# One block for the first norm and the layer-0 input projection, one block for forgetting attention, in a hybrid decoder step

## The reference, cut to what matters

```python
def rmsnorm(x, g):
    y = xf * lax.rsqrt(jnp.mean(xf * xf, axis=-1, keepdims=True) + EPS) * g

mq, mk, mv, mo, mi, mf, fq, fk, fv, ff = _split(xn @ w_in, EVEN_COLS)   # 1024 -> 28 tiles of 128 and 16 gate columns

def fox_attend(q, Fq, tq, k, v, Fk, tk):
    s = einsum(q, k) * (F_DH ** -0.5) + Fq[..., :, None] - Fk[..., None, :]
    s = where(tk <= tq, s, -inf)
    return einsum(softmax(s), v)
```

## Time and profile before

| | |
|---|---|
| median of 3 runs | 1648.03 us (1643.51 to 1653.4) |
| the profiled execution | 1647.61 us |
| its span in the trace | 1645.8 us |
| mean granted TensorE clock over the span | 0.961 |
| TensorE busy | 1555.1 us, 94% |
| input block, to the first instruction of the norm | 0 to 19.6 us |
| norm and projection (28 tiles) | 19.6 to about 219 us |
| forgetting attention, three blocks | about 350 to 472 us |

### The profile page before, as it was taken

One profiled execution on the slowest core, in us unless ns is written; L12 is line 12 of the kernel. 1 busy time (PEld: TensorE's weight loads), 2 busy tenths in 40 slices (PEclk: granted clock), 3 DMA queues, 4 the chain that ended last, 5 costly groups with the idle time before them and its releaser, 6 DMA issues. The chain is left out here.

```text
span 1645.8 us, 31029 instructions
## 1 busy us (share of the span) xinstructions
PE 1555.1 (94%) x11869; PEld 1449.7 (88%) x11869; DVE 1002.6 (61%) x1667; ACT 627.1 (38%) x1106; POOL 289.6 (18%) x313
## 2 busy tenths in 40 slices
PE   7999989988889999999999899999898999999997
PEld 5999976666659899999999899987598999999996
DVE  5332364643645989888532677635659988886325
ACT  4111231434524445555421332236334355555211
POOL 1421000400000035444000000012200254441000
PEclk8999999879999999999999999999699999999999
DMA  5223133677452023333433222230430323325221
GB/s 146 81 79 90 51 97 92 214 224 240 133 175 76 26 78 103 102 91 89 114 85 89 84 74 78 91 103 3 121 91 12 92 78 103 102 76 141 73 68 55
DMA packets 225796, 161.14 MB, mean 98 GB/s; under 512 B 17885, under 2 KB 206025, under 8 KB 225696
## 3 DMA queue, kind: packets, MB, share of 16 engines
q1 hardware_dynamic: 222416, 157.94, 33.1%
q0 software_dynamic: 3280, 1.85, 0.5%
HBM read 150.13 MB, written 9.89 MB: 97 GB/s over the span
## 5 line engine op out<-in xcount | busy, mean ns | idle before, releaser
L2327 ACT CAST w_high<-ring 128x1024 fp32r<-128x1024 f32 (+1 forms) x68 | 81.5, 1199 | 315.0 <-PE psum L2045 306.8
L2638 DVE TENSOR_TENSOR w_low<-ring,w_high 128x1024 fp32r<-128x1024 f32 (+1 forms) x68 | 97.3, 1430 | 92.4 <-ACT w_high L2327 92.4
L2161 PE MATMUL psum<-t_high,piece_high 128*128 128x280 f32 (+1 forms) x512 | 149.0, 291 | 4.1 <-ACT first_product L2463 2.5
L2162 PE MATMUL psum<-t_low,piece_high 128*128 128x280 f32 (+1 forms) x512 | 148.5, 290 | 0.0
L2163 PE MATMUL psum<-t_high,piece_low 128*128 128x280 f32 (+1 forms) x512 | 148.1, 289 | 0.0
L2428 ACT CAST piece_high<-ring 128x512 fp32r<-128x512 f32 x160 | 98.7, 622 | 75.7 <-PE psum L2163 48.4
L2161 PE MATMUL psum<-b_high,piece_high 128*128 128x280 f32 (+1 forms) x384 | 111.8, 291 | 2.1 <-DVE hidden_b L2820 2.1
L2162 PE MATMUL psum<-b_low,piece_high 128*128 128x280 f32 (+1 forms) x384 | 111.6, 291 | 0.0
L2163 PE MATMUL psum<-b_high,piece_low 128*128 128x280 f32 (+1 forms) x384 | 111.3, 290 | 0.0
L2161 PEld LDWEIGHTS psum<-t_high,piece_high 128*128 128x128 f32 x512 | 96.4, 188 | 5.0 <-ACT first_product L2463 2.9
L2163 PEld LDWEIGHTS psum<-t_high,piece_low 128*128 128x128 f32 x512 | 96.5, 188 | 0.0
(11 more groups left out here) (562 smaller groups left out, 4576.8 us busy)
## 6 DMA issues: line engine op xcount, KB each, us to landing
ring<-in_ffn_wd SPq DMA_DIRECT2D x16, 1408.0 KB, 7.1
ring<-in_ffn_wg SPq DMA_DIRECT2D x40, 512.0 KB, 4.0
ring<-in_ffn_wu SPq DMA_DIRECT2D x40, 512.0 KB, 5.2
ring<-in_w_in_even SPq DMA_DIRECT2D x14, 1024.0 KB, 5.3
ring<-in_w_in_odd SPq DMA_DIRECT2D x12, 1024.0 KB, 5.2
ring<-in_cache_fox_k SPq DMA_DIRECT2D x44, 256.0 KB, 4.3
projected<-in_cache_fox_v SPq DMA_DIRECT2D x28, 256.0 KB, 3.1
projected<-in_cache_fox_k SPq DMA_DIRECT2D x20, 256.0 KB, 3.8
```

The source lines that it names most:

```text
L2161: mm(bank, wh[:, k], xh[:, k, :], start=(j in (0, 1, 3) and k == 0), stop=False, skip_group_check=True)
L2162: mm(bank, wh[:, k], xl[:, k, :], start=False, stop=False, skip_group_check=True)
L2327: nc.scalar.copy(dst, src).then_inc(w_hi[p], 1)
L2638: v.tensor_tensor(dst, src, high_.bitcast(F32), ALU.subtract).then_inc(w_lo[p], 1)
```

## The change

**First stage.** The norm and the two projections become one block. `norm` goes away, and `project` returns one program for each engine, which the block calls one after the other. ScalarE makes the eight high parts and two weight pieces, then all eight squares. VectorE makes the eight low parts and the two weight pieces, then adds the eight squares up into one chunk (seven additions). TensorE begins its first tile chunk by chunk as the parts come, does the second, then two matmuls with ones for the sums, then the third and the fourth. The first turn is written out, the loop begins with the second. GpSimd makes no squares. The eight constants are loaded at the head of this block instead of the input block. The waits for constants and gate weights, which stood at the end of SP's program in the norm block, now stand with GpSimd's gather and with ScalarE's and VectorE's use of the gate weights. The gate products go to banks 4 and 5, behind the last use of the third tile's banks; the third tile of `even_b` waits until they are read.

**Second stage.** The three blocks of forgetting attention become one. New semaphores take the place of the block ends: TensorE's first `scores` waits for the maxima in `rows_h`, the first product with values for the copied scores of the past and for the ones beside the values; `past_maximum` and SP's loads over the keys' place wait for the copied scores (`s_S`). The probabilities of the first group are turned before the values, those of the second between the fourth and the fifth page of the first group. VectorE copies the first group's probabilities ahead of its last reciprocal. `close_fox_sems` moves behind the whole.

The diff, cut to its core:

```diff
+            def tile(i, tl, as_normed=False):
+                slot, p = tl // 2, tl % 2
+                pe.wait_ge(low_done[p], i * 2 + (s0 + slot + 1))
+                pe.wait_ge(tile_free[tl], i + free0[tl])
+                if normed and tl == 3:
+                    pe.wait_ge(n_root2, 2)
+                if pe_first is not None and tl == 2:
+                    pe.wait_ge(s_gv, 1)
...
+                    if as_normed:
+                        pe.wait_ge(n_high, k + 1)
+                    for w, m, end in ((w_high, x_high, 0), (w_high, x_low, 0), (w_low, x_high, 1)):
+                        if as_normed and m is x_low:
+                            pe.wait_ge(n_low, k + 1)
...
+            if pe_first is not None:
+                pe.wait_ge(tile_free[2], free0[2])
+                pe_first(pe)
+            if normed:
+                tile(0, 0, True)
+                tile(0, 1)
+                pe.wait_ge(n_acc, KC - 1)
+                for half in range(2):
+                    nc.tensor.matmul(banks[6 + half][:, 0:HALF], ones[:, :], normed[:, 0, half * HALF:(half + 1) * HALF],
+                                     start=True, stop=True).then_inc(n_sum, 1)
+                tile(0, 2)
+                tile(0, 3)
+            with pe.Fori(start, iters) as i:
+                for tl in range(4):
+                    tile(i, tl)
...
+            if normed:
+                for k in range(KC):
+                    nc.scalar.mul(x(k)[0], h[:, k, :], gain(0, 0, k)).then_inc(n_high, 1)
+                    if k in (0, 3):
+                        split_high(act, 0, 0, k // 3)
+                for k in range(KC):
+                    nc.scalar.activation(normed[:, k, :], h[:, k, :], ACT.Square).then_inc(n_sqa, 1)
+                split_high(act, 0, 1, 0)
+                nc.scalar.activation(eps[:, 1:2], eps[:, 0:1], ACT.Sqrt)
+                split_high(act, 0, 1, 1)
+                for half in range(2):
+                    act.wait_ge(n_sum, half + 1)
+                    nc.scalar.activation(rstd[:, half * HALF:(half + 1) * HALF], banks[6 + half][:, 0:HALF],
+                                         ACT.Sqrt, bias=eps[:, 0:1], scale=1.0 / D).then_inc(n_root2, 1)
...
+            if normed:
+                for k in range(KC):
+                    dve.wait_ge(n_high, k + 1)
+                    x_high, x_low = x(k)
+                    v.scalar_tensor_tensor(out=x_low, in0=h[:, k, :], scalar=gain(0, 0, k), in1=x_high.bitcast(F32),
+                                           op0=ALU.mult, op1=ALU.subtract).then_inc(n_low, 1)
+                    if k in (0, 3):
+                        split_low(dve, 0, 0, k // 3)
+                for k in range(1, KC):
+                    dve.wait_ge(n_sqa, k + 1)
+                    if k > 1:
+                        dve.wait_ge(n_acc, k - 1)
+                    v.tensor_tensor(normed[:, 0, :], normed[:, 0, :], normed[:, k, :], ALU.add).then_inc(n_acc, 1)
+                split_low(dve, 0, 1, 0)
+                split_low(dve, 0, 1, 1)
+                for half in range(2):
+                    dve.wait_ge(n_root2, half + 1)
+                    v.reciprocal(rstd[:, half * HALF:(half + 1) * HALF], rstd[:, half * HALF:(half + 1) * HALF])
+                v.drain()
...
+
+    def load_constants(sp):
         for dst, name in ((tri_ts, "tri_ts"), (tri_st, "tri_st"), (small, "small"), (smask, "smask")):
...
     def gather_lf(pool):
+        pool.wait_ge(s_const, 16 * 8)
...
     def gate_weights_high(act):
+        act.wait_ge(s_gw, 16 * 7)
...
     def gate_weights_low(dve):
+        dve.wait_ge(s_gw, 16 * 7)
...
     def gate_products(pe):
+        pe.wait_ge(s_gl0, 1)
...
-                    last = nc.tensor.matmul(banks[6 + half][0:96, 0:HALF], w[:, k, :],
+                    last = nc.tensor.matmul(banks[4 + half][0:96, 0:HALF], w[:, k, :],
...
-    norm(None, None, (0, 0), proj[:, 0:KC * T].rearrange("p (k t) -> p k t", k=KC), xn, splitters(1, KC, pieces),
-         load_gate_weights, zero_gate_weights)
...
-    project(even_a, 1, 4, KC, chunk(xn), Pt, 0, pieces, then=even_b, beside=gather_lf, normed=True,
-            following=(1, KC, False), act_first=gate_weights_high, dve_first=gate_weights_low)
-    project(even_b, 1, 3, KC, chunk(xn), Pt, 16, pieces, beside=reorder_lf, scaled=True, split=True,
-            pe_first=gate_products, dve_first=gate_logits, act_last=(log_sigmoid_by_scalar, gates_by_scalar),
-            dve_last=(log_sigmoid_by_vector, gates_by_vector), dve_after=keep_cumulated, bank_free=(s_gv, 1))
+    sync_a, tensor_a, scalar_a, vector_a = project(
+        even_a, 4, KC, chunk(xn), Pt, 0, pieces, then=even_b, following=True, normed=Pt,
+        act_first=gate_weights_high, dve_first=gate_weights_low)
+    sync_b, tensor_b, scalar_b, vector_b = project(
+        even_b, 3, KC, chunk(xn), Pt, 16, pieces, pe_first=gate_products, dve_first=gate_logits,
+        act_last=(log_sigmoid_by_scalar, gates_by_scalar), dve_last=(log_sigmoid_by_vector, gates_by_vector),
+        dve_after=keep_cumulated)
+    with nc.Block() as block:
...
+        def _(sp):
+            load_constants(sp)
+            load_gate_weights(sp)
+            sync_a(sp)
+            sync_b(sp)
...
+        def _(pe):
+            tensor_a(pe)
...
+        def _(pool):
+            zero_gate_weights(pool)
+            gather_lf(pool)
+            reorder_lf(pool)
...
+            sp.wait_ge(s_S, 2)
+            load_v(sp, 25, 20)
...
+            sp.wait_ge(s_fp, 2 * 4 * per_pair)
+            load_v(sp, 55, 2)
+            sp.wait_ge(v_used, 3)
+            load_v(sp, AFTER_USE, 2 * 32 - AFTER_USE)
+            sp.wait_ge(v_used, PAGES)
+            prefetch(sp, out_even)
...
+            pe.wait_ge(s_less_max, 2)
+            scores(0)
...
+                if p == 0:
+                    pe.wait_ge(s_S, 2)
+                    pe.wait_ge(s_one, 1)
...
+            def probs_turned(g):
+                b0 = 4 * g
+                pe.wait_ge(s_x2, g + 1)
+                if g:
+                    pe.wait_ge(s_fo, 16)
+                    pe.wait_ge(s_fd, 16)
...
+            probs_turned(0)
+            for g in range(2):
+                for e in range(2):
+                    pe.wait_ge(s_t2c[e], g + 1)
+                for pg in range(PAGES + 1):
+                    values(g, pg)
+                    if g == 0 and pg == 3:
+                        probs_turned(1)
+                    if g and pg == 3:
+                        out_turned(0)
+            out_turned(1)
...
+                    if c == 3 and r == 1:
+                        probs_copied(0)
...
-    close_fox_sems()
-
```

More of the change, by code:

```diff
@@ new lines, in project @@
+    def project(unit, iters, kc, x, dst, first, pieces, then=None, following=None, normed=None, pe_first=None, act_first=None,
+                dve_first=None, act_last=None, dve_last=None, dve_after=None):
+        full0, free0 = list(full_n), list(free_n)
+        s0 = split_n[0]
+        split_high, split_low, part = splitters(1, kc, pieces)
+        high, low = pieces
+        sent[0] += 16 * iters
+        split_n[0] += 2 * iters
+        for tl in range(4):
+            full_n[tl] += iters
+            free_n[tl] += iters
+        next_high, next_low, _ = splitters(1, kc, pieces) if following else (None,) * 3
+        start = 1 if normed else 0
@@ new lines, in by_tensor @@
+        def by_tensor(pe):
+            def tile(i, tl, as_normed=False):
[6 more added lines that the diff above has]
+                    pe.wait_ge(s_gv, 1)
+                w_high, w_low = part(high, p), part(low, p)
+                for k in range(kc):
+                    x_high, x_low = x(k)
[5 more added lines that the diff above has]
+                        for half in range(2):
+                            last = nc.tensor.matmul(banks[2 * tl + half][:, 0:HALF], w[:, k, :],
+                                                    m[:, half * HALF:(half + 1) * HALF],
+                                                    start=(k == 0 and w is w_high and m is x_high),
+                                                    stop=(k == kc - 1 and end == 1))
+                last.then_inc(tile_full[tl], 1)
+            if pe_first is not None:
[11 more added lines that the diff above has]
+            with pe.Fori(start, iters) as i:
+                for tl in range(4):
+                    tile(i, tl)
@@ L502, in transposes @@
         tr_n[1] += len(jobs) // 2
-    (n_sqa, n_sqp, n_pair, n_sum, n_root, n_y, n_h, n_high, n_sq) = (sem(x) for x in (
-        "squares_by_scalar", "squares_by_gpsimd", "square_pairs", "sum_done", "root_done", "post_normed", "residual",
-        "x_high", "h_squares"))
-    n_root2 = sem("h_root_done")
-    roots = [0]
-    posts, pres = [0], [0]
-    def sums_of_squares(pe, sq, chunks, ready, base, first_bank, done=None):
-        for j in range(chunks):
-            pe.wait_ge(ready, base + j + 1)
-            for half in range(2):
```

(17 more changed lines are left out.)

716 lines of the change are left out of this document (249 added, 467 removed).

## The result

The changed kernel takes 1630.1 us in the median of eight runs (1628.5 to 1635.2), the kernel before 1651.3 in the median of all 76 runs on record (1643.0 to 1657.6). In the first comparison the ratio was 0.989, with a 95% interval of 0.9864 to 0.9917; in the second, with more runs of before, 0.9882 (0.9852 to 0.9913). So the change makes the kernel 1.1 to 1.2% faster. The forecast was 1622, the range 1615 to 1630: the direction was right, the time is 8.3 us over the forecast and 0.1 us outside the range, and the gain is 21.2 us where 26.2 were forecast.

The account below looks back on a forecast made before the run. TensorE, busy 94% of the span, sets the pace, so time is won where it idles or runs at its lower clock. Gains 10.5 + 5.9 + 5.4 + 4.4 = 26.2 from 1647.6 give 1621.4, called 1622 against the median; range 1615 to 1630.

Parts of the forecast that it names:

- Step 1: Norm and projection: first tile starts chunk by chunk, sums follow the second; fourth tile ends at 48.4, gain 10.5 us.
- the first tile did not crawl: Rival at the projection's start: waits in each chunk keep TensorE at 1.2 GHz into the second tile; 1627 us, chance 0.12.
- Step 2: Gate products between `even_a` and `even_b`: they follow the last tile without gap at full clock, gain 5.9 us.
- Step 3: Forgetting attention, entry into the softmax part: TensorE waits only for the maxima, no block end; gain 5.4 us.
- Step 4: Forgetting attention, samples' values: transposes follow the last product directly, so values begin earlier; gain 4.4 us.
- the rival taken from the Trainium skill: Forgetting attention: transposes let the clock fall, first group's values partly at half rate, 2 us lost; 1624 us, chance 0.08.
- a grant under 1.00 in the steady part: Rival over the whole span: longer unbroken work makes the chip grant less clock, say 1660 us; chance 0.02.
- the low ends: The four steps' smallest gains, 6.8 + 5.6 + 4.2 + 2 = 18.6 us, or 1629 us.

Follow-up runs that it names:

- start_warm7: The kernel before with only the first-stage change, and seven instead of four products of constants ahead of the mLSTM heads: 1634.6 us, ratio 0.9903 to before.
- `warm` runs: The changed kernel with five, six or seven instead of four products of constants ahead of the mLSTM heads: 1626.7, 1630.2 and 1626.0 us.
- held kernels: Both kernels with the mLSTM heads' tiles reordered and the row of four-column products split in two: changed kernel 1626.9 us, kernel before 1645.8 us.

## Why the prediction was right in its parts and wrong in its sum

**Step 1, the start: right.** 10.5 us were said, 58.92 - 47.43 = 11.5 came in the profiled pair, 1 us of it because the input block ended earlier in this execution (15.35 against 16.35). Over all profiles with the old start (five) and the new one (nine), the fourth tile is drained 57.3 - 47.2 = 10.1 us earlier. TensorE stood at the first product 1.6 us earlier than said, at 1.2 GHz as said (0.66 in the microsecond from 24, then 1.00). VectorE's additions ended at 30.7, ahead of the 33 said; the first tile did not crawl.

**Step 2, the gate products: right.** 5.9 said; the first drain of `even_b` is 17.45 us earlier, 6.0 more than the fourth tile. Over the same five and nine profiles, the gates come 199.7 - 184.1 = 15.6 us earlier, against 16.4 said for both steps.

**Step 3, the entry: right.** 5.4 said, 13.48 - 8.84 = 4.6 in the means of six and eight profiles. The step had ScalarE load its table right behind its copy; it loads it only when the first scores are there (386.27, 0.39 us idle), and TensorE waits 1.45 us for the exponential.

**Step 4, the samples' values: right.** 4.4 said; 82.85 - 78.13 = 4.7 in the means. The first values stand 2.0 us behind the start of the transposes, and no fall of the clock follows the transposes in that stretch, so the rival taken from the Trainium skill ("TensorE: Matmul & The Clock Gate", Part 4: PE-mode transpose) did not come; each group's transposes last only 1.2 us, so this tests that rule little. The prediction's own ground for counting transposes was misread: from the start of the input block TensorE multiplies constants, and it transposes only from 10.77 to 16.31. The granted clock stayed at 1.00 through those 5.5 us and fell at 18.82 (0.91 in the microsecond from 18), so the conclusion stands for them.

**The sum: wrong.** "10.5 + 5.9 + 5.4 + 4.4 = 26.2 from the profiled 1647.6" assumed that what the change doesn't touch takes as long as in that one execution. This term was put at nothing without a reason, and it is the step that failed. In the profiled pair the steps came to 17.5 + 4.8 + 3.3 = 25.6 us, and the rest took 8.4 more: 10.2 in the mLSTM heads and the block behind them, less what other stretches gave. No rival priced this: those on the clock asked about the first tile, the transposes and a grant under 1.00 in the steady part, and none of these came. The profiled execution of before was 3.7 us under the median of all runs, and its heads held a clock that the other five profiles without an edit there lost.

Against the medians, the 8.3 us between 1621.8 and 1630.1 have three parts. The base was 3.3 too low: three runs gave 1648.0, all 76 give 1651.3. The steps gave 15.6 + 4.6 + 4.7 = 24.9 in the means, 1.3 less than 26.2. And the medians lie only 21.2 apart, so 3.7 were lost in stretches that the change doesn't touch. Two of these are longer in the profiles of the changed parts. With unaltered heads, the heads and the block behind take 60.1, 55.8 and 60.1 with the new start, 49.9, 55.8 and 55.8 with the old one, and `start_warm7` and the `warm` runs show that what runs ahead of them changes this. From the out-projection to the end, the eight profiles with merged forgetting attention take 1159.1 to 1166.4, 1163.4 in the mean, the six without 1158.7 to 1162.3, 1161.0 in the mean; there the clock is at 1.2 GHz for 52.5 us in the shortest and 66.7 us in the longest. But these are few executions, and which pattern a run without a profile fell on isn't known, so how the 3.7 us divide stays open.

The range was also narrower above than its own working: the low ends gave 1629, and the 2 or 3 us that a median may be off, which were taken off below (1618 to 1615), would have made the upper end 1631 to 1632.

## What to carry to other kernels

A gain of known steps is to be subtracted from a median of many runs, not from one execution. A stage that the change doesn't touch can still move, if TensorE's clock there hangs on what ran before it: compare two executions of the same kernel before a difference in such a stage is laid to a change. Where a row of products with few columns stands in a full stretch, it is worth trying to split it and move the parts between large ones: here that gave 3 us in the changed kernel, while one large product set into the row gave nothing that can be told. A block's end that an engine off the path reaches last is worth about the wait in the timeline: here 4.6 us where TensorE had stood still for 5.0 (392.04 to 397.05), and 4.7 where it had stood for 4.34, there with a new order of the work beside it.

## What the runs showed of the hardware that was not expected

The granted clock fell with TensorE busy 12.10 of 12.10 us; each fall in the heads came within a row of products of four columns each or at most 0.9 us behind it. I had read the clock as a matter of stops. That the few columns are the cause is argued from this and from the held kernels, not shown by itself: seven constant products ahead of the heads held the clock in heads 1 and 2 with the rows as they were. The Trainium skill ("TensorE: Matmul & The Clock Gate", Part 1: The HAM clock gate, What's actually happening) says that what watches the engine runs on by itself and does not begin anew with a kernel, so that the point of change varies. The traces agree: the same 67 products a head took 10.1 to 13.1 us, and where unaltered heads began equally long (to 0.06 us) after the clock's last return, each head's time was the same to 0.06 us. And adding work ahead of a stage (seven constant products for four, 2.6 us) took 4 us off the whole.
